# Turns of queries, keys and normed outputs moved behind the gate products in the first attention of a two-block transformer kernel

## The reference, cut to what matters

```python
def first_block(x, ...):
    h = rmsnorm(x, ln_mix_g)
    dq, dk, dv, nq, ..., ng, mg = split(h @ w_in)
    dq = rope(rmsnorm(dq, diff_q_norm_g), pos)          # [512, 8 heads, 2, 64]
    dk = rope(rmsnorm(dk, diff_k_norm_g), pos)
    y_diff = diff_attention(dq, dk, dv, lam, lambda_init, diff_subln_g)
    ...
    merge = sigmoid(mg)                                  # [512, 2, 1024]
    mixed = merge[0] * (y_diff @ w_proj_diff) + merge[1] * (y_nsa @ w_proj_nsa)
    ...

def diff_attention(q, k, v, lam, lambda_init, subln_g):
    # for each block of 128 queries, causal:
    p = softmax(q @ k.T * 64 ** -0.5)                    # two maps for each head
    a = p[0] - lam * p[1]
    o = a @ v
    return rmsnorm(o, subln_g) * (1 - lambda_init)
```

## Time and profile before

| what | us |
|---|---|
| median of 3 executions | 1842.82 |
| lowest, highest | 1839.95, 1848.19 |
| the profiled execution, its own time | 1844.95 |
| its span (first to last instruction) | 1843.1 |
| first scores of this attention | 163.12 |
| first product of the projection behind it | 286.74 |

### The profile page before, as it was taken

The page is one execution under the profiler, slowest core; times in us unless marked ns, Lnnn a source line. Parts: engine busy times, 40 slices in busy tenths (PEclk is TensorE's granted clock), DMA queues, the critical chain, the costliest instruction groups (busy, mean ns, idle before and its releaser), DMA issues.

```text
span 1843.1 us, 24707 instructions
## 1 busy us (share of the span) xinstructions
PE 1713.8 (93%) x9390; PEld 1335.0 (72%) x9390; DVE 928.5 (50%) x1664; ACT 709.6 (39%) x1609; POOL 381.4 (21%) x515
## 2 busy tenths in 40 slices
PE   6999999998879998997999999989999989798988
PEld 5887767866745555886888888867787768686766
DVE  3785673346246665254342244244645663456661
ACT  4334662212246664223332133133315552434550
POOL 5441331012125552020000000000103330022320
PEclk9999998999979999998999999989999999898979
DMA  6222004323012223332222233232230004130111
GB/s 179 71 91 90 24 24 131 109 69 114 1 41 58 63 62 99 105 100 70 88 96 92 91 100 106 92 114 72 88 93 24 25 24 160 46 99 17 47 47 46
DMA packets 107156, 141.37 MB, mean 77 GB/s; under 512 B 30300, under 2 KB 55156, under 8 KB 106800
## 3 DMA queue, kind: packets, MB, share of 16 engines
q1 hardware_dynamic: 105984, 139.10, 23.7%
q0 software_dynamic: 992, 0.86, 0.4%
q10 hardware_dynamic: 80, 0.02, 0.0%
HBM read 125.24 MB, written 4.24 MB: 70 GB/s over the span
## 4 chain that ended last, share of the span: by engine, by line
PE 77%; DVE 9%; ACT 9%; issue 3%; POOL 1%; DMA 0%; ACTq 0%; POOLq 0%; DVEq 0%
PE ps L1840 54%; PE ps L2285 3%; PE ps L1832 2%; PE ps L2260 2%; PE ps L2236 2%; PE ps L2062 2%; PE ps L2168 2%; PE ps L2083 2%; ACT pbd L856 1%; PE ps L2098 1%; DVE nm L1349 1%; ACT pb L800 1%; DVE qkt L1367 1%; DVE spl L1057 1%; ACT qkt L877 1%
## 5 line engine op out<-in xcount | busy, mean ns | idle before, releaser
L1840 PE MATMUL ps<-spl,ht 128*128 128x512 f32 x2496 | 582.9, 396 | 20.1 <-DVE xk L1542 8.5
L1840 PEld LDWEIGHTS ps<-spl,ht 128*128 128x128 f32 x2496 | 477.6, 192 | 122.9 <-DVE xk L1542 9.0
L1080 DVE TENSOR_TENSOR spl<-raw,spl 128x1024 fp32r<-128x1024 f32 x168 | 220.5, 1355 | 477.0 <-ACT spl L680 477.0
L680 ACT ACTIVATE spl<-raw 128x1024 fp32r<-128x1024 f32 x168 | 168.4, 1052 | 560.5 <-PE ps L1840 534.2
L1840 PE MATMUL ps<-ht,spl 128*128 128x512 f32 x960 | 220.2, 392 | 2.0 <-DVE spl L1080 2.0
L1840 PEld LDWEIGHTS ps<-ht,spl 128*128 128x128 f32 x960 | 181.4, 189 | 40.7 <-issue 2.9
L1840 PE MATMUL ps<-spl,uu 128*128 128x512 f32 x768 | 174.4, 389 | 0.0
L1840 PEld LDWEIGHTS ps<-spl,uu 128*128 128x128 f32 x768 | 144.1, 188 | 29.9
L2285 PE MATMUL ps<-ht,spl 128*128 128x512 f32 x576 | 154.9, 408 | 0.0
L1713 POOL TENSOR_TENSOR sq<-qkv 128x2048 f32<-128x2048 f32 (+1 forms) x15 | 51.5, 3436 | 366.1 <-ACT qkv L714 351.5
L2285 PEld LDWEIGHTS ps<-ht,spl 128*128 128x128 f32 x576 | 102.7, 190 | 19.0 <-issue 0.2
(11 more groups left out here) (294 smaller groups left out, 2262.3 us busy)
## 6 DMA issues: line engine op xcount, KB each, us to landing
raw<-w_in SPq DMA_DIRECT2D x30, 1024.0 KB, 5.2
raw<-w_mlp_up SPq DMA_DIRECT2D x16, 1024.0 KB, 5.3
raw<-w_mlp_down SPq DMA_DIRECT2D x16, 1024.0 KB, 5.0
raw<-w_in_a SPq DMA_DIRECT2D x16, 1024.0 KB, 5.3
raw<-w_in_b SPq DMA_DIRECT2D x8, 1024.0 KB, 5.7
raw<-w_proj_diff SPq DMA_DIRECT2D x4, 1024.0 KB, 6.7
stq<-qkv SPq DMA_DIRECT2D x16, 256.0 KB, 2.7
stq<-qkv SPq DMA_DIRECT2D x32, 128.0 KB, 2.5
```

What stands on the lines that cost most here:

```text
L680: act.activation(SPL[:, n % 2, HI, 2 * k:2 * k + 2], RAW[:, n % 2, 2 * k:2 * k + 2], ACT.Copy).then_inc(hi_done, 4)
L1080: dve.tensor_tensor(SPL[:, n % 2, LO, 2 * k:2 * k + 2], RAW[:, n % 2, 2 * k:2 * k + 2], SPL[:, n % 2, HI, 2 * k:2 * k + 2].bitcast(F32), A ...
L1840: last = pe.matmul(PS[:, b0 + b], left[:, x], right[:, y], start=(kt == 0 and i == 0), stop=(kt == UK * g["units"] - 1 and i == 2))
```

## The change

In TensorE's program the query or key turn leaves `turn_one` and becomes a function of its own, `turn_next(n)`. It is called behind `part(m, i)`, and `back` is called behind it. The scores, values, probability transposes, all other engines and the other attentions keep their order.

```diff
--- before.py
+++ after.py
@@ -2196,6 +2196,9 @@
                         last = pe.transpose(PS[:, turn_bank(a, PT_BANK), P * i:P * i + P],
                                             PBS[a.name][n % 3][:, 0, P * i:P * i + P], IDF[:])
                     last.then_inc(s["pt_tr"], 1)
+
+                def turn_next(n):
+
                     if a.turn_with(n):
                         m, i = a.turn_with(n)
                         if i:
@@ -2317,9 +2320,12 @@
                         values_of(n - 2)
                     if 1 <= n <= a.steps:
                         turn_p(n - 1)
-                    if a.is_diff and a.back_in(n) is not None:
-                        back(a.back_in(n))
                     part(m, i)
+                    if a.is_diff:
+                        if 1 <= n <= a.steps:
+                            turn_next(n - 1)
+                        if a.back_in(n) is not None:
+                            back(a.back_in(n))
                 return back
```

## The result

The changed kernel takes 1846.66 us (median of 20 runs, 1842.61 to 1849.6), the kernel before 1843.32 (median of 20, 1839.87 to 1848.19). The ratio is 1.002, with a 95% interval of 1.0011 to 1.0028: 2.0 to 5.2 us slower. The forecast was 1.3 us slower and 1844.1, with a range of 1838 to 1850; the sign is right, the range holds, and the size is too small: 1.3 us against 3.3 us between the medians. The profiled execution took 1846.03 us with a span of 1844.2, against 1844.95 and 1843.1.

A forecast was written before the change was run, and what follows sets the result against it. The prediction took a ring of ScalarE, VectorE and GpSimd, not TensorE, to bound the attention stage. First unit 0.8 plus key turns 0.5 gave 1.3 us slower, 1844.1 us from a median of 1842.82, range 1838 to 1850.

The forecast's parts named there:

- The ring: First attention, steady units: ScalarE, VectorE and GpSimd wait in order for each other, setting 15.41 us without any TensorE piece.
- TensorE tied to it once in a unit: In the step that turns nothing, the 512-wide tile's values wait for ScalarE's copy; waits saved earlier are lost there.
- Waits are covered and come back ahead of the copied probabilities: Steady units: output-turn and key-turn waits vanish; TensorE's wait for copied probabilities grows from 0.28 to a full microsecond.
- Query turn, slack 0.10 us, no cost: Later units: moved query turn is readable at 238.79, ScalarE takes the queries at 238.89; no cost, but narrowly.
- Key turn, five times 0.1 us: Five later units: products wait for the tanh, keys come 0.08 us late; taken as 0.1 each, 0.5 us together.
- Output turn, no cost: Five steady units: turn comes about 0.8 us later, ends over 1.2 us before ScalarE's copied probabilities; no cost.
- First unit, 0.8 us: First unit: late query and key turns delay ScalarE and the maximum; 0.8 us taken, bounds 0.55 and 0.9.
- The delay is passed on whole.: Behind the attention's last side product: order as before, so the 1.3 us reaches the kernel's whole time.
- The range: Whole kernel, 1838 to 1850 us: bounds of the terms, turns on the ring, and a median from an 8 us spread.
- TensorE-bound: Rival, steady units: TensorE is the bound and all its waits come back, 1.44 us a unit, 7.2 in five; chance 0.08.
- The clock rival: Rival, steady units: gathered waits make TensorE's clock fall; 48 us slower in five units, 1892 us; chance 0.04.
- The turns did not become part of the ring: Rival, five units: query turn joins key turn on the ring, 0.3 us each, 3 us more, about 1847; chance 0.09.

The follow-up runs named there:

- e3: Kernel before, its order kept, with half of the gate products of tiles 1 to 7 left out; profile only: unit 15.40 us.
- e7: Kernel before, TensorE's order kept, with VectorE's low half of gate weights, sums of squares and output scaling moved into idle time: 1835.21 us against 1843.96, ratio 0.9957.
- e2: Kernel before with only the turn of the normed output moved behind the products: 1845.36 us against 1844.46, ratio 1.0008.
- e1: The change, but with unit 2's two turns left ahead of the products: 1844.52 us against 1844.46 for the kernel before, ratio 1.0003.
- e6: Kernel before with only unit 2's two turns (query and key) moved behind the products: 1847.69 us against 1843.96, ratio 1.0017.
- e9: Kernel before, no turn moved, with two waited-for copies of a constant on ScalarE ahead of unit 2's query half: 1847.31 us against 1843.84, ratio 1.0016.
- e4: The changed order with half of the gate products of tiles 1 to 7 left out; profile only: stage 124.11 us against 123.64 in e3.
- the run at 0.933: One run of the kernel before, nothing changed, with a recorded clock of 0.933, far off the others of its time: 1846.69 us.
- the late kernels: The change (both times), e6, e9 and e9's variant with four copies, against the kernel before: 2 of 68 runs under 1843 us, before 26 of 78.

## Why the prediction was right, and where its size was off

- **The ring, and TensorE tied to it once in a unit.** Shown: units of 15.42 us with the waits covered, 15.40 with half of the products gone (e3), 14.13 with the ring cut (e7).
- **Waits are covered and come back ahead of the copied probabilities.** As stated: 4.8 us in five units, 0.96 in each, where a full microsecond was forecast.
- **Query turn, slack 0.10 us, no cost.** As stated; the slack was 0.26, since the products start 0.14 us behind the transposes of the probabilities and the turn 1.48 behind the products, where 0.22 and 1.55 were taken.
- **Key turn, five times 0.1 us.** The wait for the tanh came as worked out. The cost did not: 0 to 0.02 us a unit. The term that was mis-sized is the 1.55 us of six products, which was read with scores behind them; with a turn behind them they take 1.49, and that is most of the 0.08 us of lateness that was forecast. The time comes back as 0.53 us from a turn to the scores, where 0.35 was read from a turn to the products, but nothing of the ring waits there.
- **Output turn, no cost.** As stated (e2).
- **First unit, 0.8 us.** Right in kind (e1 and e6), measured 0.61 in the unit and 0.66 in the stage. Six products ahead of a turn take 1.46 us here where 1.55 was taken, and they start 0.07 to 0.08 us sooner behind the transposes of the probabilities than the turn did; so the query turn holds ScalarE for 0.53 instead of 0.68 us, and the key turn for 0.64 instead of 0.81. The stage lost 0.66 us where 1.3 were forecast.
- **"The delay is passed on whole."** This step failed. 0.6 us went into what follows and about 3 us came out: profiles show longer stretches at the low clock behind later waits of TensorE, and e9 shows that a delay alone, without any moved turn, can cost as much. The term left out is larger than all those summed.
- **The range.** That it holds is owed to its width and not to the sum. The bounds of the terms, 0.55 to 2.4 us, laid on the median of the kernel before (1843.32), end at 1845.7; 1846.66 lies in the range only because it takes in a spread of 8 us and a rival. The forecast of 1.3 us lies between two errors of opposite sign: the stage lost half of it, and the rest of the kernel added a term that it did not have.
- **The rivals.** TensorE-bound is refuted by e3. The clock rival, as it was put, a fall within the units, did not happen in the change's profile, but the clock took its share elsewhere; in e4, with gathered waits and fewer products, it came into three units of five. The turns did not become part of the ring: units of 15.42 to 15.44 us.

Open: why a delay of 0.6 us costs about 3 us, and whether one of 2.6 us costs more or less than its length. Only one profile for each kernel is there, and the 96 products vary from 23.21 to 24.80 us in them without a plain relation to the delay. At an equal mean clock (lines of one slope through all runs, time against mean clock, 0.93 us for 0.001, without the run at 0.933) the late kernels were still 1.3 to 1.8 us above before, so the mean clock does not tell all of it. That the low clock is what makes the rest of the 3 us is therefore argued from single profiles and not shown by an experiment.

## What to carry to other kernels

Before covering a wait, follow the chain of waits over one whole period: if the waiting engine has no piece in it, its waits are its spare time and come back at the next place where it is tied to the ring. The order that paid here is the one on the ring's own engines; three operations on VectorE, moved into its own idle time behind the maxima and the reciprocals, gave 8.8 us (ratio 0.9957) where covered waits on TensorE gave none. And the first period of a pipeline, where the other engines are not yet behind, has to be worked out by itself: it was the only place where the moved turns were late by more than 0.02 us.

## What the hardware showed that was not expected

- A delay of half a microsecond at 178 us (1.1 us over the stage) made the kernel about 3 us slower, one of 2.6 us did not make it measurably slower: ratios 1.0016 (1.0007 to 1.0026) and 1.0006 (0.9996 to 1.0016). In this kernel a change of a stage by some tenths of a microsecond could not be read back from the whole time to better than about 3 us.
- Behind the same wait of 4.25 us, 96 products took between 23.21 and 24.80 us, depending on how long the granted clock stayed at 0.50 of full speed (1.2 GHz).
- The length of the last gap of TensorE does not tell whether the clock falls. In e4 a gap of 1.49 us was followed by the low clock at 200.48 and not at 232.13, and one of 1.74 us at 185.07 was not either. In the change, gaps of 0.8 us among twice as many products were not followed by it, nor was one of 1.31 us in the kernel before.
